# Gate one-hots of every third token group scaled on ScalarE, and expert picks decoded by exclusive-or and minimum

## What is computed

```
s1, s2 = scores of a token's 8 heads against 128 + 128 keys
v1, i1 = top_k(s1, 16);  v2, i2 = top_k(s2, 16)
cand   = v1[:, None] + v2[None, :]            # 16 x 16 sums per head
sc, pos = top_k(cand, 16)                     # pos = 16 * a + b
idx    = i1[a] * 128 + i2[b]                  # the picked experts
g      = softmax(sc)                          # their gates
act    = gelu(u[idx] . t)
out    = sum over picks of g * act * v[idx]
```

## Time and profile before

| | us |
|---|---|
| median of 3 runs (3080.45 to 3082.49) | 3082.22 |
| the profiled execution | 3087.28 |
| its span | 3085.5 |
| PE busy | 3012.9 (98%) |
| DVE busy | 2278.6 (74%) |
| ACT busy | 1408.4 (46%) |
| POOL busy | 186.2 (6%) |

### The profile page before, as it was taken

The page is one execution under the profiler, slowest core; times in us unless marked ns, Lnnn a source line. Parts: engine busy times, 40 slices in busy tenths (PEclk is TensorE's granted clock), DMA queues, the critical chain, the costliest instruction groups (busy, mean ns, idle before and its releaser), DMA issues. The chain is left out here.

```text
span 3085.5 us, 49754 instructions
## 1 busy us (share of the span) xinstructions
PE 3012.9 (98%) x19430; PEld 2804.0 (91%) x19430; DVE 2278.6 (74%) x3254; ACT 1408.4 (46%) x1716; POOL 186.2 (6%) x232
## 2 busy tenths in 40 slices
PE   8999999999999999999999999999999999999998
PEld 8899889899999999999999999999787888888886
DVE  5777559999868888888888877698656656565564
ACT  4464343366445454545454455434444333333333
POOL 1000000020001111111111000000000000000000
PEclk9999999999999999999999999999999999999999
DMA  6443454456768999999999874544444555555553
GB/s 233 169 146 137 155 203 146 175 195 230 253 253 307 342 349 361 345 350 349 350 341 351 321 271 171 185 170 159 156 177 150 190 191 184 194 184 189 189 188 136
DMA packets 102144, 705.54 MB, mean 229 GB/s; under 512 B 13016, under 2 KB 13040, under 8 KB 18464
## 3 DMA queue, kind: packets, MB, share of 16 engines
q1 hardware_dynamic: 78272, 562.07, 49.9%
q0 software_dynamic: 21872, 128.10, 11.9%
q10 hardware_dynamic: 1872, 13.63, 1.1%
HBM read 685.46 MB, written 18.24 MB: 228 GB/s over the span
## 5 line engine op out<-in xcount | busy, mean ns | idle before, releaser
L1118 DVE TENSOR_TENSOR w_lo<-raw,w_hi 128x2048 fp32r<-128x2048 f32 x532 | 1219.2, 2292 | 454.8 <-ACT w_hi L683 430.2
L1944 PE MATMUL bank<-a_both,w_hi 128*128 128x416 f32 (+1 forms) x3840 | 1225.4, 377 | 8.6 <-DVE w_lo L1118 5.0
L1945 PE MATMUL bank<-a_both,w_lo 128*128 128x208 f32 (+1 forms) x4096 | 1040.6, 264 | 0.0
L683 ACT ACTIVATE w_hi<-raw 128x2048 fp32r<-128x2048 f32 x308 | 588.7, 1911 | 505.3 <-PE bank L1976 362.8
L1945 PEld LDWEIGHTS bank<-a_both,w_lo 128*128 128x128 f32 x4096 | 779.7, 190 | 7.1
L1944 PEld LDWEIGHTS bank<-a_both,w_hi 128*128 128x128 f32 x3840 | 722.6, 188 | 63.2 <-issue 9.0
L1922 PE MATMUL bank<-a_both,w_hi 128*128 128x256 f32 (+1 forms) x1984 | 573.0, 289 | 22.7 <-DVE w_lo L1118 15.4
L696 ACT ACTIVATE w_hi<-raw 128x1536 fp32r<-128x1536 f32 x224 | 333.8, 1490 | 506.5 <-PE bank L1945 502.7
L1923 PE MATMUL bank<-a_both,w_hi 128*128 128x256 f32 (+1 forms) x1984 | 560.4, 282 | 0.0
L1924 PE MATMUL bank<-a_both,w_lo 128*128 128x256 f32 (+1 forms) x1984 | 560.2, 282 | 0.0
L1922 PEld LDWEIGHTS bank<-a_both,w_hi 128*128 128x128 f32 x1984 | 384.0, 194 | 30.2 <-issue 13.4
(11 more groups left out here) (331 smaller groups left out, 2542.5 us busy)
## 6 DMA issues: line engine op xcount, KB each, us to landing
raw<-stream_dram SPq DMA_DIRECT2D x532, 1024.0 KB
gates_scratch<-stage ACTq DMA_DIRECT2D x13, 1024.0 KB, 4.4
gbuf<-gates_scratch POOLq DMA_DIRECT2D x30, 416.0 KB, 6.8
x<-x_dram SPq DMA_DIRECT2D x4, 512.0 KB, 6.6
x_scratch<-x POOLq DMA_DIRECT2D x1, 2048.0 KB, 11.3
mem<-mem_dram POOLq DMA_DIRECT2D x1, 2048.0 KB, 10.3
xm<-x_scratch POOLq DMA_DIRECT2D x1, 2048.0 KB, 12.2
out_dram<-x SPq DMA_DIRECT2D x4, 512.0 KB, 4.0
```

Of the source, the lines that this page charges most:

```text
L683: eng.activation(w_hi[k % SPLIT][:, :], raw[:, k % RAW, :], ACT.Copy).then_inc(hi_done, 1)
L1118: eng.tensor_tensor(w_lo[k % SPLIT][:, :], raw[:, k % RAW, :], w_hi[k % SPLIT][:, :].bitcast(F32), ALU.subtract).then_inc(split_done, 1)
L1944: mm(o, hi[:, ks], pair, start=kt == 0, stop=False)
L1945: inst = mm(o2, lo[:, ks], pair[:, 0, :], start=False, stop=False, skip_group_check=True)
```

## The change

The picks are decoded with whole numbers: the keys' indices get their slot number times 128 or-ed in (`top_x`), a and b are shifted left by 7 (`posab`), one exclusive-or of the two gives, for the slot that is picked, the index alone, and for each other slot at least 128 (`differ`), and the minimum over 16 slots is the pick. The float copies, the comparison and the product go. ACT's two Exp stand inside u0, behind the w_hi of its units 8 and 12. DVE's softmax steps stand ahead of the last `fill()`s instead of behind them, and the last one of all is left to the loop of the groups.

The groups begin in unit 0, with three of them after k-tiles 8, 11 and 15; units 1 to 9 have five, unit 10 has four and is the last. `picks_turn` stands at the start of unit 0.

For each third group (q % 3 == 1, 17 of 52) DVE makes `pick_a` as a plain one-hot of four tokens in one instruction, and ACT multiplies each token's tile in place by its gate (a copy with a scale pointer, `gate_picks`), just ahead of the evict of the group before. PE waits for each of these by `oha_act`.

```diff
--- before.py
+++ after.py
@@ -218,7 +218,7 @@
         act0 = at("act0", [P, KT, T], F32, work_at)
         wide = at("wide", [P, D], F32, work_at)
         cand = at("cand", [P, 2, TT, 256], F32, work_at + 24576)
-        onehot = at("onehot", [P, PICKS, TOPK], F32, work_at + 24576)
+        differ = at("differ", [P, PICKS, TOPK], U32, work_at + 24576)
         pick_a = at("pick_a", [P, 8, P], F32, work_at + 24576)
         pick_b = at("pick_b", [P, 8, P], F32, work_at + 28672)
         gbuf = at("gbuf", [P, 4, TBLOCKS, 4 * TBLOCK], F32, work_at + 16384)
@@ -226,11 +226,11 @@
 
         top_v = [at(f"top_v{tt}", [P, 16, TOPK], F32, o) for tt, o in enumerate((pk, wdtf_at))]
         top_i = [at(f"top_i{tt}", [P, 16, TOPK], U32, o + 1024) for tt, o in enumerate((pk, wdtf_at))]
-        top_f = at("top_f", [P, 16, TOPK], F32, pk + 2048)
+        top_x = at("top_x", [P, 16, TOPK], U32, pk + 2048)
         sc = at("sc", [P, TT, PEER_HEADS, TOPK], F32, pk + 3072)
         pos = [at(f"pos{tt}", [P, PEER_HEADS, TOPK], U32, pk + o) for tt, o in enumerate((4096, 12928))]
         posab = at("posab", [P, 2, PICKS], U32, pk + 4608)
-        posf = at("posf", [P, 2, PICKS], F32, pk + 5632)
+        slot_x = at("slot_x", [P, TOPK], U32, pk + 5632)
         picked = at("picked", [P, TT, 3, PICKS], F32, pk + 6656)
         pickT = at("pickT", [P, 3, T], F32, pk + 9728)
         gsum = at("gsum", [P, TT, PEER_HEADS], F32, pk + 12800)
@@ -353,6 +353,8 @@
         picks_done = sem("picks_done")
         pickT_psum = sem("pickT_psum")
         oha_done = sem("oha_done")
+        oha_raw = sem("oha_raw")
+        oha_act = sem("oha_act")
         ohb_done = sem("ohb_done")
         g_mm = sem("g_mm")
         g_evict = sem("g_evict")
@@ -427,8 +429,10 @@
         EB = 32
 
         GROUPS = TD // 4
+        BY_ACT = [q for q in range(GROUPS) if q % 3 == 1]
+        BY_DVE = [q for q in range(GROUPS) if q not in BY_ACT]
         GATES_AFTER = (2, 5, 8, 11, 15)
-        GATES_UNIT = {1 + q // 5: [n for n in range(GROUPS) if n // 5 == q // 5] for q in range(GROUPS)}
+        GATES_UNIT = {(q + 2) // 5: [n for n in range(GROUPS) if (n + 2) // 5 == (q + 2) // 5] for q in range(GROUPS)}
 
         LAST_GROUP = max(GATES_UNIT)
 
@@ -701,7 +705,7 @@
                 eng.wait_ge(mm_done, u + 1)
                 eng.activation(w_hi[k % SPLIT][:, PART:UNIT], raw[:, k % RAW, PART:UNIT], ACT.Copy).then_inc(hi_done, 1)
 
-            def feature(name, n, first, evict, r=None, unroll=False):
+            def feature(name, n, first, evict, r=None, unroll=False, between=None):
                 u0 = UNIT0[name] + first
                 if unroll:
 
@@ -712,6 +716,8 @@
                         evict(k // 4, k % 4)
                         if k > 0:
                             ahead(u0 + k, (r, RU))
+                        if between:
+                            between(k)
                     return
                 with eng.Fori(0, n // 4) as g:
                     for j in range(4):
@@ -894,15 +900,29 @@
             def gelu0(g, j):
                 eng.activation(act0[:, g * 4 + j, 0:TD], bank[j][:, 0:TD], ACT.Gelu).then_inc(bank_free, 1)
             eng.wait_ge(s_xw, 16)
-            feature("u0", 16, 0, gelu0, unroll=True)
-
-            for tt in range(TT):
-                eng.wait_ge(sm_dve, tt + 1)
-                eng.activation(sc[:, tt, :, :], sc[:, tt, :, :], ACT.Exp).then_inc(sm_act, 1)
-
+            def gate_exp(k):
+
+                if k in (8, 12):
+                    tt = (k - 8) // 4
+                    eng.wait_ge(sm_dve, tt + 1)
+                    eng.activation(sc[:, tt, :, :], sc[:, tt, :, :], ACT.Exp).then_inc(sm_act, 1)
+
+            feature("u0", 16, 0, gelu0, unroll=True, between=gate_exp)
+
+
+            def gate_picks(q):
+
+                j = 4 * (q % 2)
+                eng.wait_ge(oha_raw, BY_ACT.index(q) + 1)
+                for i in range(4):
+                    t = G + 4 * q + i
+                    eng.activation(pick_a[:, j + i, :], pick_a[:, j + i, :], ACT.Copy, scale=pickT[:, 2, t:t + 1])\
+                        .then_inc(oha_act, 1)
 
             def evict_group(q):
 
+                if q + 1 in BY_ACT:
+                    gate_picks(q + 1)
                 block, half = q // 4, (q // 4) % 2
                 if q % 4 == 0 and block >= 2:
                     eng.wait_ge(g_write[half], 16 * (block // 2))
@@ -1516,33 +1536,32 @@
                     eng.wait_ge(s_wide2, 16)
                     eng.tensor_tensor(xw[0:G, :], x[0:G, 0, :], wide2[0:G, :], ALU.mult).then_inc(xw_done, 1)
 
+            own.do(eng.tensor_scalar(slot_x[:, :], C("iota", 0, TOPK), float(PEER_KEYS), None, ALU.mult))
             for tt in range(TT):
-                own.did(eng.tensor_copy(top_f[:, :, :], top_i[tt][:, :, :]))
-                tf = top_f[:, :, :].rearrange("p (h two) k -> p h two k", two=2)
+                own.did(eng.tensor_tensor(top_x[:, :, :], top_i[tt][:, :, :],
+                                          slot_x[:, :].unsqueeze(1).to_broadcast([P, 16, TOPK]), ALU.bitwise_or))
+                tx = top_x[:, :, :].rearrange("p (h two) k -> p h two k", two=2)
 
                 own.did(eng.tensor_copy(first[:, :], sc[:, tt, :, 0]))
 
                 pf = pos[tt][:, :, :].rearrange("p h k -> p (h k)")
-                own.did(eng.tensor_scalar(posab[:, 0, :], pf, 4, None, ALU.logical_shift_right))
-                own.did(eng.tensor_scalar(posab[:, 1, :], pf, 15, None, ALU.bitwise_and))
+                own.did(eng.tensor_scalar(posab[:, 0, :], pf, 4, 7, ALU.logical_shift_right, ALU.logical_shift_left))
+                own.did(eng.tensor_scalar(posab[:, 1, :], pf, 15, 7, ALU.bitwise_and, ALU.logical_shift_left))
                 own.wait()
                 eng.tensor_tensor(sc[:, tt, :, :], sc[:, tt, :, :],
                                   first[:, :].unsqueeze(2).to_broadcast([P, PEER_HEADS, TOPK]),
                                   ALU.subtract).then_inc(sm_dve, 1)
-                own.do(eng.tensor_copy(posf[:, :, :], posab[:, :, :]))
                 for half in range(2):
                     if waiting:
                         fill()
-                    own.do(eng.tensor_tensor(onehot[:, :, :], C("iota", 0, TOPK).unsqueeze(1).to_broadcast([P, PICKS, TOPK]),
-                                             posf[:, half, :].unsqueeze(2).to_broadcast([P, PICKS, TOPK]), ALU.is_equal))
-                    oh = onehot[:, :, :].rearrange("p (h k) a -> p h k a", h=PEER_HEADS)
-                    own.do(eng.tensor_tensor(oh, oh, tf[:, :, half, :].unsqueeze(2).to_broadcast([P, PEER_HEADS, TOPK, TOPK]),
-                                             ALU.mult))
+                    own.do(eng.tensor_tensor(
+                        differ[:, :, :].rearrange("p (h k) a -> p h k a", h=PEER_HEADS),
+                        posab[:, half, :].rearrange("p (h k) -> p h k", h=PEER_HEADS).unsqueeze(3)
+                        .to_broadcast([P, PEER_HEADS, TOPK, TOPK]),
+                        tx[:, :, half, :].unsqueeze(2).to_broadcast([P, PEER_HEADS, TOPK, TOPK]), ALU.bitwise_xor))
                     if waiting:
                         fill()
-                    own.do(eng.tensor_reduce(picked[:, tt, half, :], onehot[:, :, :], AX.X, ALU.add))
-            while waiting:
-                fill()
+                    own.do(eng.tensor_reduce(picked[:, tt, half, :], differ[:, :, :], AX.X, ALU.min))
             for tt in range(TT):
                 eng.wait_ge(sm_act, tt + 1)
                 own.do(eng.tensor_reduce(gsum[:, tt, :], sc[:, tt, :, :], AX.X, ALU.add))
@@ -1550,6 +1569,8 @@
                 eng.tensor_tensor(picked[:, tt, 2, :].rearrange("p (h k) -> p h k", h=PEER_HEADS), sc[:, tt, :, :],
                                   gsum[:, tt, :].unsqueeze(2).to_broadcast([P, PEER_HEADS, TOPK]), ALU.mult)\
                     .then_inc(picks_done, 1)
+            while len(waiting) > 1:
+                fill()
 
 
             own.do(eng.scalar_tensor_tensor(pick_f[:, :], picked[0:G, 0, 0, :], float(PEER_KEYS), picked[0:G, 0, 1, :],
@@ -1569,12 +1590,17 @@
                 eng.tensor_tensor(pick_b[:, j:j + 4, :], C("iota").unsqueeze(1).to_broadcast([P, 4, P]),
                                   pickT[:, 1, G + 4 * q:G + 4 * q + 4].unsqueeze(2).to_broadcast([P, 4, P]),
                                   ALU.is_equal).then_inc(ohb_done, 1)
+                if q in BY_ACT:
+                    eng.tensor_tensor(pick_a[:, j:j + 4, :], C("iota").unsqueeze(1).to_broadcast([P, 4, P]),
+                                      pickT[:, 0, G + 4 * q:G + 4 * q + 4].unsqueeze(2).to_broadcast([P, 4, P]),
+                                      ALU.is_equal).then_inc(oha_raw, 1)
+                    return
                 for i in range(4):
                     t = G + 4 * q + i
                     eng.tensor_scalar(pick_a[:, j + i, :], C("iota"), pickT[:, 0, t:t + 1], pickT[:, 2, t:t + 1],
```

(18 more changed lines are left out.)

## The result

In 20 runs each, interleaved, the changed kernel takes **3085.74 us** (median; 3083.73 to 3090.11) and the kernel before 3081.88 (3078.57 to 3084.29): a ratio of **1.0015, interval 1.0008 to 1.0021**. That is slower by 3.9 us, inside the 0.2% that was called the same, and 0.5 us from the 3085.2 of the forecast. The profiled execution took 3090.11 (span 3088.3), 2.8 more than the profiled one of before.

What follows compares the result with a forecast made beforehand. A loop through DVE, not only its busy time, was taken to set the gate units. Losses of 18.0 plus a 1.5 clock fall, 19.5 against 16.5, gave 3082.2+3.0 = 3085.2 us; 8-in-10 range 3069 to 3092.

Steps and rivals of the forecast that it cites:

- What bounds it: In units with five gate groups, a loop through DVE makes the unit 10.35 us; PE alone needs 9.83.
- The ledger: Sum of PE time lost from u0's unit 7 to u1's last unit: 16.5 us before, 19.5 after with one clock fall.
- units 2 to 9: These units of u1 take 89.6 us against PE's own 78.6: 11.0 lost, before 4.0.
- the wait before unit 12: First gating stands ahead of unit 12's w_lo on DVE and waits for the scratch write: 2.95 us lost with restart.
- the one fall that the forecast had: One fall of the granted clock, at the wait before unit 12, costing 1.5 us.
- The decoding: In u0, picks by xor and minimum drop four products, 9.2 us of DVE; PE sets the pace, 4.4 us back.
- The rival at twice the time: Xor and unsigned minimum take twice the time, so DVE holds up u0: 3096.7 us; chance 0.05.
- The exps: Exp inside u0 with two table round trips, each done 5.1 us after the unit's end, under 5.36: cost nothing.
- That rival: Table loads inside u0 each hold ACT 1.4 us more, PE waits 1.8 twice: 3.6 more, 3088.8 us; chance 0.03.
- The hand-over: Groups gated by ACT reach PE 1.85 us after DVE starts them, not 1.18; three unit kinds, up to 11.91 us.
- The clock rival: Clock also falls at the long waits in units 1, 2, 5, 8: 6.0 us more, 3091.2 us; chance 0.17.
- The rival that all hand-over is free: DVE and ACT run ahead, so PE finds every group ready: 12.5 us back, 3069.7 us; chance 0.30.

Runs made afterwards that it cites:

- the first experiment: Changed kernel with all 52 groups' gates put on by DVE again, the rest of the change kept: 3077.07 us, ratio 0.9984.
- the four places: All gates by DVE and w_lo order changed, but ACT gates ten groups at one position per unit: second 3071.67, fourth 3077.58, first 3079.75, third 3081.74 us.
- the w_lo order changed: Changed kernel with unit 12's w_lo ahead of the first gating on DVE, each later gating behind a w_lo: 3080.91 us, ratio 0.9996.
- one unchanged program: Changed kernel with all gates by DVE and the w_lo order changed, run twice: 3069.61 us (5 runs) and 3072.72 us (6 runs).

## Why the prediction was right, point by point

**What bounds it** held. A loop through DVE, PE and the one-hot tiles sets the unit, and the kernel with all gates by DVE, where that loop is untouched, has the 10.35 of before to 0.01.

**The ledger** of lost time was made against 16.5 us before. Term by term, forecast and measured: the late w_lo and unit 0, 1.1 and at most 0.2 (PE busy 58.00 of the 58.00 us to 640); unit 1, 2.1 and 2.0 (11.80 long); units 2 to 9, 11.0 and 12.2 (90.81 long), 1.5 of it a clock fall in unit 5 that the forecast did not have; unit 10, 0.9 and 0.9; the wait before unit 12, 2.95 and 2.8; the fall behind it, the one fall that the forecast had, 1.5 and 3.3. Together 19.5 and 21.3. The stretch's end moved from 782.10 to 786.73, by 4.6, where 3.0 was forecast. Behind it PE waits 3.4 us for w_lo where it waited 5.0 (784 to 1820 us; 1.79 for 3.62 at the start of u2), so POOL's first load of the next stage, at 1816.6 before, stands 3.1 later, and the end 2.8. That the total came within 0.5 is therefore partly luck: **the term that was mis-sized is the clock**, 4.8 where 1.5 stood; the other terms together came 1.6 under theirs, 0.9 of it in unit 0, and the shorter wait in u2, which the forecast did not have, took off 1.8 more.

**The decoding** gave the 4.4 that were written, at a price per instruction (2.285) that was the lower bound, and keeps them when it is alone. The rival at twice the time fell.

**The exps** cost nothing, as forecast: the rows above show 1.28 for each load and an exp 1.29 behind its start. The Trainium skill (ScalarE: Activation LUTs, What ACT_TABLE_LOAD costs) adds a drain of about 1380 ns to every switch. The trace does not agree: from the first load (596.97) to gelu (600.17) are 3.20, of which the two loads and the exp take 2.87, and in the kernel with the exps behind u0 gelu starts 1.29 after its load does (648.12, 649.41). That rival fell too.

**The hand-over** was right in each kind of unit: first and fourth 11.29 and 10.9 (forecast 11.29, 10.94), second and fifth 10.0 to 10.4 (10.19 to 10.53), third 11.90 where the clock stays (11.91). The pitch of a 128x128 activation with a scale pointer was taken as 0.29 between bounds of 0.22 and 0.39, and four took 1.28 with 0.39 to 0.40 for each: 0.30. The Trainium skill (ScalarE: Activation LUTs, What ACT_TABLE_LOAD costs) gives 186 ns, 0.833 ns an element, 93 ns a pointer and 93 ns of overlap; by these figures an estimate for this shape is 386 ns for one and 293 in a row. Trace and page agree (mean of one 389 ns in the trace).

**The clock rival** was right about the mechanism and wrong about the count. It asked for falls at four waits. Waits of 1.70 came three times, in units 2, 5 and 8, and one, in unit 5, was followed by a fall. The wait of 2.65 before unit 12, which this rival did not list and where the forecast had its one fall, had the longest low stretch. The hand-over waits of units 1, 2, 5 and 8 brought one fall in all, where that rival needed three more than before.

**The rival that all hand-over is free** fell with the first experiment and, from the other side, with the four places: it would have needed slack at every group, and of the four that were tried only the second has it.

## What to carry to other kernels

Work taken off a busy engine can be worth nothing, or less, where the engine is one station of a ring: before moving a step to a second engine, work out when its consumer wants it and when the longer route delivers it, for each place in the cycle; here one place of the four tried had the room, and 0.29 us in hand was not enough for a hand-over of 0.67. Put work that waits for a DMA round trip behind, not ahead of, the step that feeds the matrix engine next: here that order cost 4 us. And count the low clock behind a long wait as a cost of its own, from 1.5 to 3.3 us a time here.

## What the runs showed of the hardware

PE waits of equal length are not equally followed by the low clock. In before and in the kernel with the decoding alone the wait of 1.72 was followed by a stretch of 0.41 per matmul of some 3.2 us. In the changed kernel, of three waits of 1.70, one was, and by 697.6 the matmuls were at 0.27 again. With the w_lo order changed, two of the same three were, in units 2 and 8. Before unit 12 the longer wait had the shorter fall: behind 3.31 (all by DVE) the matmuls were slow from 755.3 to 758.6, behind 2.65 (after) from 761.8 to 768.4. What decides it is open; no run here was made to find out.

An exclusive-or of 128x2048 unsigned words and a minimum over them, written as floats, cost DVE what the same shapes of floats cost (2.285 and 2.279). Whole-kernel medians of one unchanged program moved by 3 us between two sets of runs, while the stretch under study agreed to 0.1 in the two profiled executions. The granted clock between 2300 and 2420 us was 0.97 in some profiles and 1.00 in others, though the work there is the same. In the two of that program it was 1.00 and 0.97, and the one with 0.97 was the faster by 1.4 us, so this does not explain the 3 us.
